# Modulation of the second block by 48 reducing passes on VectorE, and a rearranged norm of the last token tile

## What is computed

```python
def rmsnorm(x, g):
    return x * rsqrt(mean(x * x, axis=-1) + EPS) * g

# end of the first block
x = x + merged @ w_out
x = rmsnorm(x, norm_final)

# second block; c is (1, 1024), mod_w is (1024, 6144)
sh1, sc1, g1, sh2, sc2, g2 = split(silu(c) @ mod_w + mod_b, 6)
x = x + g1 * hyena_mix(rmsnorm(x, norm_g[0]) * (1 + sc1) + sh1)
x = x + g2 * conv_ffn(rmsnorm(x, norm_g[1]) * (1 + sc2) + sh2)
return rmsnorm(x, final_g)
```

## Time and profile before

| | |
|---|---|
| median of three runs | 1061.9 us (1061.57 to 1061.93) |
| the profiled execution | 1061.37 us |
| its span in the profile | 1059.3 us |
| TensorE busy (matmul) | 1040.0 us, 98% |
| VectorE, ScalarE, GpSimd busy | 63%, 40%, 51% |
| granted TensorE clock | full speed in all 40 slices |

### The profile page before, as it was taken

The page is one execution under the profiler, slowest core; times in us unless marked ns, Lnnn a source line. Parts: engine busy times, 40 slices in busy tenths (PEclk is TensorE's granted clock), DMA queues, the critical chain, the costliest instruction groups (busy, mean ns, idle before and its releaser), DMA issues.

```text
span 1059.3 us, 13471 instructions
## 1 busy us (share of the span) xinstructions
PE 1040.0 (98%) x4968; PEld 856.4 (81%) x4968; DVE 665.7 (63%) x1007; ACT 418.6 (40%) x687; POOL 543.7 (51%) x401
## 2 busy tenths in 40 slices
PE   7999999999999999999999999999999999999996
PEld 5889887877877888778888888778888888888885
DVE  5663776866499765985788847386666666520503
ACT  6223547665554243644444342442323223221222
POOL 1688895999200064234444346535465545553641
PEclk9999999999999999999999999999999999999999
DMA  6446454342446922212322113303222232223222
GB/s 257 164 168 225 133 187 153 90 163 70 179 159 238 379 104 100 93 67 80 110 83 84 54 42 155 143 33 146 87 80 79 103 135 79 80 80 135 104 80 79
DMA packets 19611, 131.92 MB, mean 125 GB/s; under 512 B 3411, under 2 KB 3811, under 8 KB 13030
## 3 DMA queue, kind: packets, MB, share of 16 engines
q1 hardware_dynamic: 8784, 92.62, 23.2%
q0 software_dynamic: 6560, 27.27, 8.0%
q10 hardware_dynamic: 4214, 11.30, 2.8%
HBM read 124.90 MB, written 6.30 MB: 124 GB/s over the span
## 4 chain that ended last, share of the span: by engine, by line
PE 95%; DVE 2%; ACT 1%; DMA 1%; issue 0%; POOL 0%; SPq 0%; POOLq 0%; ACTq 0%; DVEq 0%
PE bank L505 81%; PE bank L496 7%; PE bank L511 3%; PE bank L752 1%; PE bank L746 1%; DMA x_sb<-x_in 1%; PE bank L904 1%; PE bank L741 1%; DVE arena L2178 0%; DVE arena L2181 0%; PE bank L913 0%; PE bank L753 0%; PE bank L869 0%; ACT arena L1189 0%; DVE arena L2214 0%
## 5 line engine op out<-in xcount | busy, mean ns | idle before, releaser
L1730 POOL TENSOR_TENSOR ring_parts<-ring,ring_parts 128x1024 fp32r<-128x1024 f32 x102 | 248.7, 2442 | 266.3 <-ACT ring_parts L1189 263.5
L505 PE MATMUL bank<-hT_parts,ring_parts 128*128 128x512 f32 x1344 | 339.2, 393 | 0.8 <-ACT hT_parts L1518 0.8
L1189 ACT ACTIVATE ring_parts<-ring 128x1024 fp32r<-128x1024 f32 (+2 forms) x163 | 168.6, 1043 | 383.7 <-PE bank L505 219.9
L505 PEld LDWEIGHTS bank<-hT_parts,ring_parts 128*128 128x128 f32 x1344 | 249.6, 188 | 54.7 <-ACT hT_parts L1518 2.4
L505 PE MATMUL bank<-ring_parts,hT_parts 128*128 128x512 f32 (+1 forms) x672 | 171.6, 379 | 1.0 <-POOL ring_parts L1730 0.6
L505 PE MATMUL bank<-ring_parts,arena_parts 128*128 128x512 f32 (+1 forms) x736 | 172.4, 386 | 0.0
L505 PEld LDWEIGHTS bank<-ring_parts,arena_parts 128*128 128x128 f32 x736 | 136.6, 188 | 27.9 <-DVE arena L2416 0.3
L505 PE MATMUL bank<-arena_parts,ring_parts 128*128 128x512 f32 x592 | 148.0, 391 | 0.3 <-DVE arena_parts L2285 0.3
L505 PEld LDWEIGHTS bank<-ring_parts,hT_parts 128*128 128x128 f32 x672 | 122.4, 188 | 22.8 <-POOL ring_parts L1730 1.0
L2521 DVE SCALAR_TENSOR_TENSOR arena<-bank,small,arena 128x441 f32<-128x441 f32 (+2 forms) x176 | 122.3, 695 | 24.6 <-DVE arena L2521 1.7
L505 PEld LDWEIGHTS bank<-arena_parts,ring_parts 128*128 128x128 f32 x592 | 111.0, 188 | 25.4 <-DVE arena_parts L2285 2.1
(11 more groups left out here) (223 smaller groups left out, 1100.5 us busy)
## 6 DMA issues: line engine op xcount, KB each, us to landing
ring<-weights_in SPq DMA_DIRECT2D x39, 2048.0 KB, 8.0
arena<-mod_w_in POOLq DMA_DIRECT2D x32, 512.0 KB, 4.1
arena<-mod_w_in POOLq DMA_DIRECT2D x8, 1024.0 KB, 5.5
x_sb<-x_in SPq DMA_DIRECT2D x4, 512.0 KB, 5.7
ring<-weights_in SPq DMA_DIRECT2D x4, 512.0 KB, 8.5
mod_spill<-mod_part POOLq DMA_DIRECT2D x16, 128.0 KB, 2.1
x_sb<-x_in ACTq DMA_DIRECT2D x4, 512.0 KB, 12.2
arena<-mod_spill ACTq DMA_DIRECT2D x1, 2048.0 KB, 10.6
```

Of the source, the lines that this page charges most:

```text
L505: ins = nc.tensor.matmul(out, l, r, start=start and n == 0, stop=stop and n == len(passes) - 1)
L1189: return nc.scalar.activation(out, in_, ACT.Copy)
L1730: return nc.gpsimd.tensor_tensor(part(low), low, part(high), ALU.subtract)
```

## The change

All six vectors are formed on VectorE. The weight matrix is laid out transposed, so that one output feature lies in one partition, and 48 instructions (`mod_tile`) each multiply a tile of 128x1024 by the row silu(c), spread over the partitions, and write the sum along the row into one column of `modc`. Twelve of them stand in stage 1, 28 in stages 3 and 4 (two after each of 14 pieces), and eight among the first eight merges. GpSimd only issues the loads, 0.5 MB each, four buffers deep. The gates g1 and g2 go from columns to rows through DRAM (`mod_row`) by two transfers on ScalarE's queue. TensorE's `modulation` and `gate_rows` are gone, and so is the copying out of their banks.

For the last of the four token tiles, the second norm no longer waits for the first: VectorE multiplies the tile by `norm_final` (`gain_last`), ScalarE squares both this and the tile itself, in halves, GpSimd combines the two sums to one factor, and VectorE applies it (`scale_gained`). `norm_x2` of this tile, whose result only goes to DRAM, comes after that; ScalarE waits for it before it sends the tile and goes on to `spec_first`. The padding before `arena`, the large buffer, is chosen so that its address stays as it was.

```diff
-MOD_POOL_COLS = 128
-MOD_POOL = 4 * D // MOD_POOL_COLS
-MOD_DVE_COLS = 256
-MOD_AFTER = (9, 11, 13, 15, 16, 17, 18, 19)
-ROOTS_AFTER = (11, 21, 23, 25, 27)
-PAUSE_AFTER = 17
+MOD_TILES = 6 * KD
+MOD_EARLY = 12
...
-        sb("to_line", [P, -((nc.sbuf_base + 31) // 32 * 32) % LINE // 4])
-        mod_part = sb("mod_part", [P, 2 * MOD_POOL_COLS])
-        modc = sb("modc", [P, 4 * KD])
+        sb("to_line", [P, (LINE - (nc.sbuf_base + 31) // 32 * 32) % (4 * LINE) // 4])
+        minus = sb("minus", [P, 256])
         arena = sb_twice("arena", [P, 111 * 256], [(256 * a, 256 * b) for a, b in ((0, 44), (54, 70), (70, 111))])
...
-        modw_dve = [at(65, 2048, KD), at(75, 2048, KD)]
-        modw_pool = [at(99, 1024, KD), at(103, 1024, KD)]
+        cond_row = mod_g[:, 0, :]
+        modw_early = [at(99, D), at(103, D), at(65, D), mod_g[:, 1, :]]
+        modw_late = [at(75, D), at(79, D), at(65, D), at(69, D)]
         x1_norm = at(75, TT * D, TT)
-        mod_back = at(75, 4 * D)
         rowed = at(107, N_ROWED)
         cos_t, sin_t, nsin_t = (at(109 + 0.5 * i, 128) for i in range(3))
         probs1 = [at(54, 1280), at(59, 1280)]
...
-            modulation(0)
-            gate_rows(0)
             wo_tile(0)
             wo_tile(1)
-            modulation(1)
-            gate_rows(1)
             filter_tile(0)
             wo_tile(2)
-            modulation(2)
             filter_tile(1)
...
             wo_tile(7)
-            gate_rows(2)
-            gate_rows(3)
-            modulation(3)
 
...
             for p in range(4, 15):
                 split_high(p)
+                if p == 8:
+                    wait("cond_in", 16)
+                    nc.scalar.activation(cond_row, cond_row, ACT.Silu).then_inc(sem("cond_ready"), 1)
             for i in range(8, 12):
...
             split_high(FIRST_PD + 4)
-            wait("mod_dve_done", MOD_DVE)
-            act.dma_start(mod_back, mod_spill_d).then_inc(sem("mod_back_in"), 16)
-            act.dma_start(mod_part[:], tables_d[:, 2048:2304]).then_inc(sem("tables_in"), 16)
+            act.dma_start(minus[:], tables_d[:, 2048:2304]).then_inc(sem("tables_in"), 16)
             wait("h3_ready", 1)
             act.dma_start(deltas, deltas_d.partition_broadcast(P).rearrange("p a d -> p (a d)")).then_inc(sem("filter_rows_in"), 16)
             for p in range(FIRST_PD + 5, FIRST_PD + 8):
                 split_high(p)
+            wait("mod_summed", MOD_TILES)
+            act.dma_start(at(75, 1024), tables_d[:, 0:1024]).then_inc(sem("tables_in"), 16)
 
             def wout_split(n):
                 wait("wout_sum", 2 * n + 2)
...
                 if m < 2:
                     decay_out(6 + m)
                     square_x2(m)
+            last = TT - 1
+            wait("wo_out", TT)
+            square(x_sb[:, last, 0:512], SS_L, "x1_last", 0)
             split_high(FIRST_HYZ)
-            square_x1(TT - 1)
             square_x2(TT - 2)
+            wait("gained", 1)
+            square(x_norm[:, last, 0:512], SS_L + 1, "gained", 0)
+            wait("wo_out", 2 * TT)
+            square(x_sb[:, last, 512:D], SS + last, "x1_right", 0)
+            wait("gained", 2)
+            square(x_norm[:, last, 512:D], SS2 + last, "gained_right", 0)
             split_high(FIRST_HYZ + 1)
-            square_x2(TT - 1)
+            wait("x2_ready", TT)
+            act.dma_start(spill_d[last * P:TT * P, :], x_sb[:, last, :]).then_inc(sem(f"x_in{last}"), 16)
+
+            wait("gates_ready", 1)
+            act.dma_start(mod_row_d.rearrange("a (t p) -> p (a t)", p=P), modc[:, 4 * KD:MOD_TILES],
+                          allow_slow_non_contiguous=True).then_inc(sem("mod_row_out"), 16)
 
...
                           allow_slow_non_contiguous=True).then_inc(sem("norm_cols_in"), 16)
+            wait("mod_row_out", 16)
+            act.dma_start(mod_g[:].rearrange("p a b -> p (a b)"),
+                          mod_row_d.partition_broadcast(P).rearrange("p a d -> p (a d)")).then_inc(sem("modg_in"), 16)
             act.dma_start(inv_tab, tables_d[:, 1024:2048].rearrange("p (a b) -> p a b", a=8)).then_inc(sem("tables_in"), 16)
...
-            def load_dve(j):
-                if j == 0:
-                    wait("pT_out", 4 * UNITS)
-                    wait("pv_done", 4 * UNITS)
-                elif j == 1:
-                    wait("o_ready", UNITS)
+            def load_mod(j):
+                if j < MOD_EARLY:
+                    b, buffers, name = j % len(modw_early), modw_early, "modw_early"
+                    used = j - len(modw_early) + 1
                 else:
-                    wait("mod_dve_done", j - 1)
-                a = MOD_POOL * 1024 + j * 2048
-                pool.dma_start(modw_dve[j % 2], mod_d[:, a:a + 2048].rearrange("p (k c) -> p k c", k=KD)).then_inc(sem(f"modw_in{j % 2}"), 16)
+                    b, buffers, name = (j - MOD_EARLY) % len(modw_late), modw_late, "modw_late"
+                    used = j - len(modw_late) + 1 if j >= MOD_EARLY + len(modw_late) else 0
+                if used > 0:
+                    wait("mod_summed", used)
+                pool.dma_start(buffers[b], mod_d[:, j * D:(j + 1) * D]).then_inc(sem(f"{name}{b}"), 16)
 
             def latent_roots():
...
-            wait("lambda_sums", 1)
-            load_pool(0)
-            load_pool(1)
-            wait("cond_ready", 1)
-            cb = st(CSILU, KD).unsqueeze(2).broadcast_to([P, KD, C])
-            for j in range(MOD_POOL):
-                w = modw_pool[j % 2]
-                wait(f"modw_in{j % 2}", 16 * (j // 2 + 1))
-                link(nc.gpsimd.tensor_tensor(w, w, cb, ALU.mult))
-                for n in (4, 2):
-                    link(nc.gpsimd.tensor_tensor(w[:, 0:n, :], w[:, 0:n, :], w[:, n:2 * n, :], ALU.add))
-                if j % 2 == 0 and j:
-                    wait("mod_spilled", 16 * j // 2)
-                nc.gpsimd.tensor_tensor(mod_part[:, j % 2 * C:(j % 2 + 1) * C], w[:, 0, :], w[:, 1, :],
-                                        ALU.add).then_inc(sem("mod_pool_done"), 1)
-                wait("mod_pool_done", j + 1)
-                if j % 2:
-                    pool.dma_start(mod_spill_d[:, (j - 1) * C:(j + 1) * C], mod_part[:]).then_inc(sem("mod_spilled"), 16)
-                if j + 2 < MOD_POOL:
-                    load_pool(j + 2)
...
-                if j == ROOTS_AFTER[0]:
+            chunk_landed(pool, C_DK)
+            pool.dma_start(cond_row, cond_d.partition_broadcast(P).rearrange("p a d -> p (a d)")).then_inc(sem("cond_in"), 16)
+            for j in range(MOD_EARLY):
+                load_mod(j)
+                if j == 11:
                     latent_roots()
-                if j == PAUSE_AFTER:
-                    wait("probs_ready", 4)
-                for h in range(HEADS):
-                    if j == ROOTS_AFTER[1 + h]:
-                        head_roots(h)
-            link(nc.gpsimd.memset(mod_g[:], 0.0))
-            pool.dma_start(mod_g[0:1, :, :].rearrange("p a b -> p (a b)"), mod_b_d).then_inc(sem("mod_b_in"), 16)
-            load_dve(0)
-            load_dve(1)
-            wait("o_turned", UNITS)
...
                 root_x1(m)
                 root_x2(m)
             root_x1(2)
-            root_x1(3)
+            last = TT - 1
+            wait("squares_done", squares_at("x1_last", 0))
+            link(nc.gpsimd.tensor_scalar(st(SS_L), st(SS_L), 1.0 / D, NORM_EPS, ALU.mult, ALU.add))
             root_x2(2)
-            root_x2(3)
+            wait("squares_done", squares_at("gained", 0))
+            link(nc.gpsimd.tensor_scalar(st(SS_L + 1), st(SS_L + 1), 1.0 / D, None, ALU.mult))
+            wait("squares_done", squares_at("x1_right", 0))
+            link(nc.gpsimd.tensor_scalar(st(SS_L), st(SS + last), 1.0 / D, st(SS_L), ALU.mult, ALU.add))
+            link(nc.gpsimd.tensor_scalar(st(SS_L + 1), st(SS_L), NORM_EPS, st(SS_L + 1), ALU.mult, ALU.add))
+            wait("squares_done", squares_at("gained_right", 0))
+            rsqrt_sum(RS2 + last, SS2 + last, SS_L + 1, "x2_rs")
+            nc.gpsimd.tensor_tensor(st(RS + last), st(SS_L), st(MHALF), ALU.pow).then_inc(sem("x_rs"), 1)
             wait("n2_scaled", TT)
             for p in range(FIRST_HYZ, FIRST_HYZ + PIECES):
                 split_low(p)
@@ -1950,17 +1901,6 @@
...
-            def mod_chunk(j):
-                C = MOD_DVE_COLS
-                wait(f"modw_in{j % 2}", 16 * (MOD_POOL // 2 + j // 2 + 1))
-                acc = mod_g[:].rearrange("p a b -> p (a b)")[:, j * C:(j + 1) * C]
-                w = modw_dve[j % 2]
-                for k in range(KD):
-                    ins = V.scalar_tensor_tensor(out=acc, in0=w[:, k, :], scalar=st(CSILU + k), in1=acc, op0=ALU.mult, op1=ALU.add)
-                    if k < KD - 1:
-                        link(ins)
-                ins.then_inc(sem("mod_dve_done"), 1)
...
+            def mod_tile(j):
+                if j < MOD_EARLY:
+                    b = j % len(modw_early)
```

(52 more changed lines are left out.)

90 lines of the change are left out of this document (24 added, 66 removed).

## The result

The changed kernel takes 1068.9 us, the median of four runs (1068.54 to 1069.75), against 1061.9 (1061.57 to 1061.93) for the kernel before: a ratio of 1.0065, 95% interval 1.0052 to 1.0078. It is 7.0 us slower, where I had forecast 1060.2 us and a range that ended at 1066. Its profiled execution took 1069.25 us with a span of 1067.4, 8.1 above the span before.

A forecast was written before the change was run, and what follows sets the result against it. TensorE was taken to bound the kernel (98% busy, 95% of the chain). -7.0 + 1.65 (first tile) + 0.6 (network layer) + 0.3 (merges) + 2.7 (seam) = -1.75 from 1061.37, plus 0.53 for the median: 1060.2 us, range 1055.5 to 1066.

The forecast's parts named there:

- Removed from TensorE: modulation and gate_rows leave TensorE: 10.4 us, of which 7.0 stand before wo_tile(3) and 3.4 after wo_tile(7).
- 1.65: First w_out tile behind the merges: TensorE waits 0.55 us for the eighth high part and 1.1 for a low part.
- The cost of a tile: One mod_tile on VectorE, called c: 1.38 us, low end 1.19, high end 2.57 with a second pass.
- Stage 1 and the network layer: Twelve tiles in stage 1 cost nothing; in stage 3 TensorE waits 0.6 us for the second network layer.
- The merges: Stage 4: VectorE has 3.2 us in hand against 3 to 4 us of waiting for loads; cost 0.3 us.
- rival (b): VectorE late at the merges, ending at 333.5 + 36c plus DMA waiting (c: us per tile); 1065 us, chance 0.15.
- three signs of a wrong prediction: Tile over 1.5 us; VectorE waiting over 4 us for the tiles' DMAs; ScalarE at the spectrum's copies before 452.
- The seam: Behind wo_tile(7): 2.7 us longer although 3.4 us of matmuls are gone; ScalarE's wait for norm_x2(3) ends last.
- After the seam: The gates' two transfers, the arena's padding and the moved roots cost nothing; late transfers would show at 645 us.
- (a): The seam after wo_tile(7) does not get longer, TensorE's 3.4 us come off partly or wholly: 1054 to 1057.5 us, chance 0.25.
- (c): Half rate of mod_tile on VectorE: 2.57 us a tile, merges end 39.7 us later, 1098 us; chance 0.10.

The follow-up runs named there:

- e4: The changed kernel with the eight mod_tiles among the first merges moved to stage 1 (twenty there, none among the merges): 1065.7 us.
- e2: The changed kernel with the last tile's norm done as before, so that only the modulation is changed: 1057.6 us.
- e7: The changed kernel with GpSimd's subtractions after add_abs(6) and ScalarE's wait for norm_x2(3), with its two transfers, after the second high part: 1060.0 us.
- e6: The changed kernel with twenty mod_tiles in stage 1, GpSimd's subtractions after add_abs(6), ScalarE's transfers later, add_wo(7) and gain_last(1) before norm_x2(2): 1061.3 us.

## Why the prediction was wrong

**Removed from TensorE, 10.4 us.** Right; the 120.74 us of e4, 5.2 below the kernel before, is the forecast -7.0 + 1.65 + 0.3 = -5.05 for that stretch, once VectorE is in time.

**The cost of a tile.** 1.38 forecast, measured 1.217 us and 0.08 for the read, 1.15 from the start of the one to the start of the other, so 1.22 in all. The half rate is refuted: the Trainium skill's rule (Vector Engine (DVE) Microarchitecture Reference, "Points that are easy to get wrong") does not hold for this instruction, since both sources were float32 in SBUF in 48 of 48 and none took over 1.23 us. The row of `norm_x2`, the same operation without the sum, was the better guide.

**Stage 1 and the network layer.** Forecast 0 and 0.6. The second filter layer's matmul starts 0.9 us later (301.60), but TensorE does not wait for it: the block before it takes 11.1 us in both. The 0.9 is older: 0.3 at the first matmuls, and 192 matmuls of stage 1 that took 31.05 us instead of 30.41. The new norm alone, which touches nothing there, has 31.04 as well, and e2 and e4 have 30.41, so this is not the change's.

**The merges, forecast 0.3, measured 2.7** (123.42 against the 120.74 of e4). The step that failed is the size of the wait for the loads: 3 to 4 us, set equal to what VectorE had in hand. It was 9.2 us, 5.2 of them at 350 us, where the timeline of VectorE has:

```profile
350.02 0.08 DVE L1950 DVE_READ_ACCUMULATOR arena<-arena,mod_g 128x1 f32 x1
355.32 1.23 DVE L1950 SCALAR_TENSOR_TENSOR arena<-arena,mod_g 128x1024 f32<-128x1024 f32 x1 [5.21 <-DMA arena<-mod_w_in]
```

The place (343 to 358 us) and the cause were as written, and this was rival (b)'s mechanism; waiting over 4 us was the one of the three signs of a wrong prediction that came. It was worth 2.4 us more than forecast, not enough for that rival's time: the tile is up to 0.16 us cheaper than forecast, and by rival (b)'s 36 c this gave VectorE back up to 5.8 us (an estimate). (Rival (b)'s own sum was off, too: +6.7 - 0.3 on top of a forecast of 1060.2 is 1066.6, not 1065, and lies outside the range.)

**The seam, forecast +2.7, measured +10.3.** Term by term, from the end of `wo_tile(7)`: the wait for `add_wo(7)` was forecast at 2.7 and is 2.79. The spectrum was forecast at 5.4 and takes 7.1, by the clock, but TensorE waits for ScalarE behind it anyway. `norm_x2(3)` was to end at +8.3 (453.6 - 445.28) and ends at +10.8, and **this is the step that failed: I gave it the 1.28 us of the earlier trace rows, a row that has GpSimd idle, though the change puts it behind the very scaling that lets GpSimd begin**. The projection therefore starts at +15.35, where I had +12.87. Then I let it run at its old pace, 10.8 us to the second spectrum; it took 15.9, since `input_full(0)` stood behind the lengthened `add_abs(6)`, which I did not follow at all, and since the clock was low. Together 2.5 + 5.1 = 7.6 us. The profiled execution is 9.6 us above the 1059.6 forecast for it: these 7.6, the 2.4 of the merges, 0.3 ahead of them, less 0.2 in the stretch and 0.6 behind the seam.

The price stood in the trace of the kernel before, in rows that my working did not use: `add_abs(1)` beside GpSimd's subtractions (timelines of VectorE and GpSimd, kernel before; the last row is the next `add_abs`, behind them).

```profile
417.77 2.94 DVE L2178 TENSOR_TENSOR arena<-arena 128x512 f32<-128x512 f32 x1
420.75 2.75 DVE L2181 TENSOR_TENSOR arena<-arena 128x512 f32<-128x512 f32 x1
...
424.79 0.69 DVE L2178 TENSOR_TENSOR arena<-arena 128x512 f32<-128x512 f32 x1
```

```profile
415.39 7.56 POOL L1730 TENSOR_TENSOR ring_parts<-ring,ring_parts 128x1024 fp32r<-128x1024 f32 x3 [0.20 <-ACT ring_parts L1189]
```

With 3.44, 2.94 and 2.75 for the three steps the working would have given 455.8 for ScalarE's release and some 461.5 for the end of `add_abs(6)`; with 2.9 us from there to the third transpose, as in the changed kernel, and 9.6 from it to the second spectrum, as in the kernel before, that is an estimate near 1065 us. I did write in the part on stage 1 that VectorE's subtractions had to share with GpSimd; I applied it to what GpSimd leaves, and not to what VectorE joins.

**After the seam.** Right: nothing shows at 645 us (TensorE has no wait there), and the transfers of the gates cost nothing.

**The rivals.** (a) was refuted: TensorE's 3.4 us did not come off. (c) was refuted by the price of the tile. (b) was partly at work. The mechanism that decided was none of the three.

## What to carry to other kernels

An instruction that is moved changes its neighbours: for each step that is reordered, ask what the step ahead of it now releases, and take its price from a row with that other engine at work, not from the nearest row of the same shape. And a wait of TensorE can cost more than its length: price the matmuls behind it at the lower clock as well, and try filling a gap that another engine ends.

## What the runs showed of the hardware

**VectorE waits for GpSimd where both of its inputs are in SBUF.** Beside `split_low` on GpSimd (2.36 us alone), VectorE's operation with two inputs in SBUF went from 0.69 to 2.75 to 2.94 us and from 1.28 to 3.44, that is by 2.1 to 2.3 us each, about one of GpSimd's instructions. GpSimd's grew too, to 2.5 each beside `add_abs(1)` (three in 7.56 us) and 2.6 to 2.8 in the changed kernel's seam. Operations with one input in SBUF and one in PSUM did not change; VectorE in the kernel before, while GpSimd was at work from 453.86 to 463.3:

```profile
455.09 0.69 DVE L2312 TENSOR_TENSOR arena<-bank,arena 128x512 f32<-128x512 f32 x1
```

The Trainium skill says this (SBUF — State Buffer, section "Who interferes with whom": a VectorE instruction with two SBUF inputs contends with a GpSimd instruction that reads SBUF, for an exclusive pair of ports, and one with at most one SBUF input, outside the two-port modes, does not). The trace agrees. By that rule the three instructions that now lie beside GpSimd's are each lengthened; at the 2.25 and 2.06 us that the rows of `add_abs(1)` show for one, this is an estimate of 6.5 us of VectorE's time, where 6.3 came.

**The clock after a wait.** TensorE's clock was granted at 0.50 behind gaps of 2 to 3 us in most profiles without filling, for 2 to 10 us at a time, and stayed at 1.00 in one (e7) that had gaps of 2.8, 0.8 and 1.7 us; which gap lowers it, these runs do not settle. Filling the gaps gained 1.0 to 2.9 us, of which only the 2.9 is clear of the scatter. That shorter waits can lose to longer ones (e6 against e7, 1.3 us) I had not expected; but with the gaps filled the first still takes 1059.8, no better than the second. The Trainium skill (TensorE: Matmul & The Clock Gate, Part 1) has the two levels, and matmuls at half pace at the lower one; 1.71 against 0.92 us for four agrees.

**The cost of filling.** A 128x512 matmul of float32 operands as they are takes 0.87 us, in two records; those of the products here are of the reduced type and take 0.23.
